# Reciprocal sums on a diagonal in the turning product, context tiles inside the last GLA head, and two stages that begin tile by tile of h

## What is computed

```python
p = softmax(scores)                      # MLA and NA: exp(s - max) / sum
out = einsum('bhqk,bkhd->bqhd', p, v)
h = x * (1 + sc1) + sh1                  # "plain" input of a layer of the second stack
x = layer_norm(alpha * x + g2 * mlp(x * (1 + sc2) + sh2))
merge(...) = concatenate([rms_norm(attn) * .., rms_norm(mem) * sigmoid(o)]) @ w_out   # even mixer
```

## Time and profile before

| | |
|---|---|
| median of 3 runs | 2934.42 us (2933.34 to 2937.86) |
| the profiled execution | 2933.31 us |
| its span in the profile | 2931.3 us |
| mean granted TensorE clock | 0.983 |
| TensorE busy | 2828.8 us, 97% of the span |
| VectorE busy | 2013.9 us, 69% |
| ScalarE busy | 1281.7 us, 44% |
| GpSimd busy | 339.3 us, 12% |
| chain that ended last | TensorE 80%, VectorE 11%, ScalarE 5% |

### The profile page before, as it was taken

The page is one execution under the profiler, slowest core; times in us unless marked ns, Lnnn a source line. Parts: engine busy times, 40 slices in busy tenths (PEclk is TensorE's granted clock), DMA queues, the critical chain, the costliest instruction groups (busy, mean ns, idle before and its releaser), DMA issues.

```text
span 2931.3 us, 44027 instructions
## 1 busy us (share of the span) xinstructions
PE 2828.8 (97%) x17694; PEld 2492.6 (85%) x17694; DVE 2013.9 (69%) x3397; ACT 1281.7 (44%) x2121; POOL 339.3 (12%) x380
## 2 busy tenths in 40 slices
PE   7999999998999999999999989999999999999998
PEld 6888898666888889888897889999979999887898
DVE  7789956555687656788655775666656689767764
ACT  4222244354422224222245565565455554645653
POOL 0000011322100001000011110022102210300100
PEclk8999999899999999999999999999999999999999
DMA  6666522011455534556432234455425579653453
GB/s 245 222 223 230 201 85 94 29 51 43 145 201 208 212 125 158 201 205 210 145 113 80 72 130 151 149 176 174 164 81 172 187 277 327 199 155 101 137 187 115
DMA packets 141194, 467.63 MB, mean 160 GB/s; under 512 B 27024, under 2 KB 29200, under 8 KB 140480
## 3 DMA queue, kind: packets, MB, share of 16 engines
q1 hardware_dynamic: 125440, 408.20, 41.2%
q0 software_dynamic: 15552, 56.63, 5.5%
HBM read 463.73 MB, written 1.05 MB: 159 GB/s over the span
## 4 chain that ended last, share of the span: by engine, by line
PE 80%; DVE 11%; ACT 5%; issue 2%; DMA 2%; POOL 1%; SPq 0%; ACTq 0%; DVEq 0%; POOLq 0%
PE bank L2657 24%; PE bank L2658 24%; PE bank L2659 24%; DVE sb_split_low L2061 3%; DVE sb_h_low L2148 1%; DMA sb_raw<-weights 1%; PE bank L2929 1%; PE bank L3100 1%; PE bank L2948 1%; DMA sb_ada_mlp<-ada 1%; DVE sb_temp L2075 1%; PE bank L2889 1%; DVE sb_x_res L2264 1%; DVE sb_temp L2142 1%; ACT sb_temp L1966 1%
## 5 line engine op out<-in xcount | busy, mean ns | idle before, releaser
L2657 PE MATMUL bank<-sb_h_high,sb_split_high 128*128 128x256 f32 (+1 forms) x3464 | 1116.6, 322 | 39.5 <-DVE sb_h_low L2156 16.5
L2658 PE MATMUL bank<-sb_h_low,sb_split_high 128*128 128x256 f32 (+1 forms) x3464 | 1097.8, 317 | 0.0
L2659 PE MATMUL bank<-sb_h_high,sb_split_low 128*128 128x256 f32 (+1 forms) x3464 | 1097.1, 317 | 0.0
L1646 ACT ACTIVATE sb_split_high<-sb_raw 128x1024 fp32r<-128x1024 f32 x620 | 646.4, 1051 | 306.6 <-PE bank L2659 286.2
L2061 DVE TENSOR_TENSOR sb_split_low<-sb_raw,sb_split_high 128x1024 fp32r<-128x1024 f32 x620 | 758.6, 1232 | 21.6 <-ACT sb_split_high L1646 21.5
L2657 PEld LDWEIGHTS bank<-sb_h_high,sb_split_high 128*128 128x128 f32 x3464 | 666.7, 192 | 100.9 <-issue 17.7
L2658 PEld LDWEIGHTS bank<-sb_h_low,sb_split_high 128*128 128x128 f32 x3464 | 667.8, 193 | 40.8
L2659 PEld LDWEIGHTS bank<-sb_h_high,sb_split_low 128*128 128x128 f32 x3464 | 667.0, 193 | 40.7
L2075 DVE CUSTOM_DVE_ANT_0 sb_temp<-sb_ada_ffn,sb_cond_ffn 128x1024 bf16<-128x1024 f32 x364 | 429.7, 1220 | 25.1 <-DMA sb_ada_ffn<-ada 16.0
L2657 PE MATMUL bank<-sb_hidden_high_ffn,sb_split_high 128*128 128x512 f32 (+1 forms) x830 | 280.4, 338 | 0.0
L2659 PE MATMUL bank<-sb_hidden_high_ffn,sb_split_low 128*128 128x512 f32 (+1 forms) x830 | 279.2, 336 | 0.0
(11 more groups left out here) (329 smaller groups left out, 3498.2 us busy)
## 6 DMA issues: line engine op xcount, KB each, us to landing
sb_raw<-weights SPq DMA_DIRECT2D x620, 512.0 KB, 3.4
sb_ada_ffn<-ada SPq DMA_DIRECT2D x114, 512.0 KB, 4.6
sb_ada_ffn<-ada POOLq DMA_DIRECT2D x90, 512.0 KB, 3.8
sb_ada_mlp<-ada POOLq DMA_DIRECT2D x18, 512.0 KB, 5.6
sb_ada_mlp<-ada SPq DMA_DIRECT2D x18, 512.0 KB, 5.9
sb_cond_ffn<-cond SPq DMA_DIRECT2D x3, 1024.0 KB, 5.4
sb_na_raw<-na_rpb SPq DMA_DIRECT2D x32, 96.0 KB, 6.8
sb_x_res<-tokens SPq DMA_DIRECT2D x4, 512.0 KB, 7.7
```

Source lines behind the costliest of these rows:

```text
L1646: do.activation(m.high[s % HIGHS][:, :], m.raw[s % RAWS][:, :], identity).then_inc(*act.mark("split_high", s))
L2657: do.matmul(out, ah, bh, start=start and j == 0, stop=False)
L2658: do.matmul(out, ah, bl, start=False, stop=False)
L2659: last = do.matmul(out, al, bh, start=False, stop=stop and j == len(terms) - 1)
```

## The change

Four edits. The weights of MLA and NA are no longer multiplied by the reciprocals. VectorE writes a 128 by 128 diagonal of them, and the turn is an ordinary float32 matmul with that diagonal as the moving operand. There is one diagonal for each c, so VectorE waits for the turn of the unit before. In the even mixer both spreads become a piece of their own, one unit later, and all four heads are put in unit 16. The context tiles 4 to 7 of cp00 move into units 22 to 26 of the GLA, into temps 0 to 3, and the first four pieces of `cmla_down` and of mlp1 are done tile by tile in four banks; n12 is then woven with the last three pieces only.

```diff
+def by_tile(pieces, ks=range(DT)):
+    for k in ks:
+        for first, *rest in pieces:
+            yield (*first, k, ks[0], ks[-1])
+            if k == ks[-1]:
+                yield from rest
...
-    extra[15] = extra[15] + [("even_put", "da", 0, j) for j in (0, 1)]
-    extra[16] = extra[16] + [("even_put", "da", 0, j) for j in (2, 3)]
+    extra[16] = extra[16] + [("even_put", "da", 0, j) for j in range(4)]
-    outs = [out_piece("even_out", k, 0, BOTH, ring) for k in range(4)]
-    outs += [[*even_spread("da", 0, j, ring), *out_piece("even_out", 4 + j, 0, BOTH, ring)] for j in range(2)]
-    outs += [out_piece("even_out", k, 0, BOTH, ring) for k in range(6, DT)]
+    outs = [out_piece("even_out", k, 0, BOTH, ring) for k in range(5)]
+    outs += [[step for j in range(2) for step in even_spread("da", 0, j, ring)]]
+    outs += [out_piece("even_out", k, 0, BOTH, ring) for k in range(5, DT)]
...
+    for i in range(4):
+        units[22 + i][0].append(("plain", "cp00", 4 + i, 0))
+        units[23 + i][0].append(("plain_put", "cp00", 4 + i, 0))
...
-    yield from flat([kept_warm(body[0], 9), *body[1:]])
+    yield "warm", 5, 9
+    yield from by_tile(body[:4])
+    yield from flat(body[4:])
...
-    tiles = plain_tiles("cp00", 0)
-    early = in_groups(tiles, (2,) * 7)
+    tiles = [(name, "cp00", k, 0) for name, k in skewed(4, ("plain", None, "plain_put"))]
+    early = in_groups(tiles, (2,) * 3)
-    yield from weave(down, [[], sums, [], spread, *tiles])
+    yield from by_tile(down[:4], (*range(4, DT), *range(4)))
+    yield from weave(down[4:], [sums, [], spread, *tiles])
...
+        self.diag = [self.ones, sb("diag", (P, P))]
...
+        if tag == "cp00" and k >= 4:
+            for d in range(2):
+                act.wait_ge("chunk_out", (2, d, N_CHUNKS - 1))
+        elif tag == "cp00":
+            act.wait_ge("h_low", (tag, k + 4, p))
...
         for c in range(2):
-            temp = m.temp[2 * (u % 3) + c][:, 0:n]
-            do.tensor_scalar(temp, temp, col[:, 4 + c:5 + c], None, ALU.mult)
+            if u:
+                dve.wait_ge("turned", (kind, u - 1, c))
+            do.tensor_scalar(m.diag[c][:, :], m.C("ident"), col[:, 4 + c:5 + c], None, ALU.mult)
...
-                last = do.transpose(m.bank[bank][:, kt * P:(kt + 1) * P], m.temp[2 * (u % 3) + c][:, kt * P:(kt + 1) * P], m.C("ident"))
+                last = do.matmul(m.bank[bank][:, kt * P:(kt + 1) * P], m.temp[2 * (u % 3) + c][:, kt * P:(kt + 1) * P], m.diag[c][:, :],
+                                 start=True, stop=True)
```

More of the change, by code:

```diff
@@ L1007, in order @@
     yield "gates", "odd_out"
+    yield "scales", "cp00"
     yield from flat(head[1])
@@ L1010, in order @@
     yield "scales", "n12"
-    yield "scales", "cp00"
     yield from beside_ffn11()
@@ L1387, in wait_for_x, with plain_temp @@
         lane.wait_ge("x_new", (src, k, p))
+def plain_temp(tag, k):
+    return k % (4 if tag == "cp00" else 5)
 def wait_for_h_free(lane, tag, p, k):
@@ L1710, in plain @@
         act.wait_ge("scales", tag)
-        if k >= 5:
+        if tag == "cp00" and k >= 4:
[3 more added lines that the diff above has]
+            act.wait_ge("h_low", (tag, k + 4, p))
+        elif k >= 5:
             act.wait_ge("h_low", (tag, k - 5, p))
-        do.activation(m.temp[k % 5][:, COLS[p]], m.x[:, k, COLS[p]], identity, scale=m.scales_of(tag)[:, k, p:p + 1],
+        do.activation(m.temp[plain_temp(tag, k)][:, COLS[p]], m.x[:, k, COLS[p]], identity, scale=m.scales_of(tag)[:, k, p:p + 1],
                       bias=m.mods[:, first + shift * DT + k, p:p + 1]).then_inc(*act.mark("plain", (tag, k, p)))
@@ L1722, in plain_put @@
         act.wait_ge("plain", (tag, k, p))
-        put_high(tag, k, p, m.temp[k % 5][:, COLS[p]])
+        put_high(tag, k, p, m.temp[plain_temp(tag, k)][:, COLS[p]])
     def layer_norm(tag, p, ks=range(DT)):
@@ L2159, in plain_put @@
     def plain_put(tag, k, p):
-        low_of(tag, k, p, m.temp[k % 5][:, COLS[p]])
+        low_of(tag, k, p, m.temp[plain_temp(tag, k)][:, COLS[p]])
         last_low[0] = tag, k, p
@@ L2578, in na_scores, with pair_normalise @@
         pair_max("na", u, T)
-    def pair_normalise(kind, u, n):
+    def pair_normalise(kind, u):
         col = m.cols[u % 6]
@@ L2585, in pair_normalise @@
         for c in range(2):
-            temp = m.temp[2 * (u % 3) + c][:, 0:n]
-            do.tensor_scalar(temp, temp, col[:, 4 + c:5 + c], None, ALU.mult).then_inc(*dve.mark("weights", (kind, u, c)))
+            if u:
+                dve.wait_ge("turned", (kind, u - 1, c))
+            do.tensor_scalar(m.diag[c][:, :], m.C("ident"), col[:, 4 + c:5 + c], None, ALU.mult).then_inc(
+                *dve.mark("weights", (kind, u, c)))
     def cmla_normalise(u):
-        pair_normalise("cmla", u, NC_TOK)
+        pair_normalise("cmla", u)
     def mla_normalise(u):
-        pair_normalise("mla", u, T)
+        pair_normalise("mla", u)
     def na_normalise(u):
-        pair_normalise("na", u, T)
+        pair_normalise("na", u)
     def weigh_put(kind, hd):
@@ L2664, in columns_of, with h_product @@
         return m.high[s % HIGHS][:, c], m.low[s % RAWS][:, c]
[L2666 to L2671, removed]
+    def h_product(bank, tag, s, p, keys, at=None, first=0, end=DT - 1):
+        if at in (None, first):
+            free(bank)
+            pe.wait_ge("split_low", s)
+        last = products(m.bank[bank][:, 0:T if p == BOTH else NC_TOK], [
+            (("h_low", (tag, k, p) if p in H_PARTS.get(tag, (0, 1)) else (tag, k)), *columns_of(s, k), *m.h_term(k, p))
+            for k in (range(DT) if at is None else (at,))], start=at in (None, first), stop=at in (None, end))
+        if at in (None, end):
+            last.then_inc(*pe.mark("gemm", *keys))
     def rstd_spread(tag, p):
@@ L2755, in small_sum, with up @@
         read[bank] = "mean", (tag, p)
-    def up(f, h, ab, p, bank):
+    def up(f, h, ab, p, bank, *at):
         s = PLACE[up_slab(f, h, ab)]
-        h_product(bank, H_OF[f], s, p).then_inc(*pe.mark("gemm", ("up", f, h, ab, p), s))
+        h_product(bank, H_OF[f], s, p, [("up", f, h, ab, p), s], *at)
         read[bank] = ("relu_squared" if n_up(f) == 1 else "hidden_raw" if ab else "silu"), (f, h, p)
@@ L2780, in down, with fm @@
         read[bank] = "x_new", ("x", f, c, k, p)
-    def fm(name, j, p, bank):
+    def fm(name, j, p, bank, *at):
         s = PLACE[fm_slab(name, j)]
-        h_product(bank, H_OF[name], s, p).then_inc(*pe.mark("gemm", ("fm", name, j, p), s))
+        h_product(bank, H_OF[name], s, p, [("fm", name, j, p), s], *at)
         read[bank] = fm_signal(name, j), (name, j, p)
@@ L2798, in out @@
         else:
-            s = PLACE[SLAB0[name] + k]
-            last = h_product(bank, tag, s, p)
-            keys.append(s)
+            assert False
         last.then_inc(*pe.mark("gemm", *keys))
```

## The result

The changed kernel takes 2945.73 us (median of 7 runs, 2942.75 to 2950.19) against 2936.98 us for the kernel before on the same chip (7 runs, 2933.34 to 2941.10). The ratio is 1.0036, with a 95% interval of 1.0025 to 1.0047: 10.6 us slower (7.3 to 13.8). The prediction had 2948.5 and "slower".

A forecast was written before the change was run, and what follows sets the result against it. TensorE, busy for 97% of the span, was taken as the bound, so added passes are paid wherever it never waits. 23.8 - 4.2 - 4.0 - 1.5 + 1.1 = +15.2 us on 2933.3 gives 2948.5, range 2936 to 2957.

The forecast's parts named there:

- The turn's records: Turn in cmla, MLA and NA: 448 records for 224 at 0.106 us each, 23.8 us more on TensorE.
- What NA absorbs: NA: 4.2 of TensorE's 7.6 us idle time come back, 2.6 in three waits and 1.6 in four late units.
- the prediction's last sentence: Forecast is wrong if the turns keep their pace, or if TensorE's idle time in NA falls to nothing.
- The new wait on VectorE: MLA: VectorE stands up to 2.8 us in three of eight units for the previous unit's turn; costed at nothing.
- That rival: VectorE's new wait becomes TensorE's: 8.4 us added in MLA, giving 2957; chance 0.11.
- The even mixer's end: Before 706: first and third of three waits go, 1.99 + 2.06 = 4.0 us gained; the middle 2.85 stays.
- The context's first projection: 1694 to 1737: 6.9 us won, 4.4 given back before ffn11, 1.0 off for moved work; 1.5 gained.
- The split does not stall: In cmla_down the low split has nothing before it but ScalarE's copy, so no stall.
- mlp1: Last feed-forward: 0.9 us won at the start, 2.0 stall before the fifth piece for a low split; loses 1.1.
- The turn is not free: Answers the rival that the turn costs no more than before, giving 2927.3, faster; chance 0.07.
- its plain matmul is not four transposes long: Answers the rival that the plain product is four transposes long: 71 us in place of 23.8, 2996; chance 0.02.
- The gains come in full: Rival: NA swallows 7.6 us, even mixer wins 10.1, projection 2.5, mlp1 even: +3.6, 2936.9; chance 0.12.

The follow-up runs named there:

- e6: Kernel before with each transpose of the turning product issued twice into the same place, VectorE's multiplications unchanged: ratio 1.0044, +12.9 us (9.4 to 16.7).
- e10: Kernel before with the turning product alone changed, but four diagonals in place of two, so VectorE waits for the turn two units before: ratio 1.0051, +15.0 us.
- e2: Kernel before with the even mixer's end alone changed (four puts in unit 16, both spreads as a piece of their own): ratio 0.9972, -8.2 us.
- e8: Kernel before with mlp1's first three pieces tile by tile, otherwise as before: ratio 0.9987, -3.8 us (-6.5 to -1.5).
- e4: Kernel before with the beginning of mlp1 alone changed (first four pieces tile by tile, nine warm matmuls on bank 5): ratio 1.0006, +1.8 us.
- e1: Kernel before with the turning product alone changed (diagonals, two-record matmuls): ratio 1.0052, +15.3 us (11.4 to 19.1).
- the single kernels: Four kernels, each the kernel before with one part of the change alone (turn, even mixer, context, mlp1): +15.3, -8.2, +0.9 and +1.8 us.
- e7: Kernel before with cp00 tiles 4 to 7 in the GLA, but cmla_down piece by piece and n12 woven as before: ratio 0.9976, -7.0 us.
- e9: Kernel before with the edits of e2, e7 and e8 together, the turn as before: ratio 0.9937, -18.5 us, median 2919.08 us.

## Why the prediction was right, step by step

The sign came out and the size roughly (+15.2 predicted, +10.6 measured). The turn's term was 4 us too high and the even mixer's gain 4 us too small, which both make the forecast too high; the context's term was 2 us too good and mlp1's 1 us, which hid part of it. That the sum lies no further off is to this extent luck, and one step, what NA absorbs, failed by a sign that the prediction itself had named.

- **The turn's records.** Right. 448 records, one more for each transpose. 23.8 us was predicted; at 0.117 us a record in MLA and 0.112 in NA, in place of 0.106, it is 3.8 + 7.5 + 14.3 = 25.6. A turn of MLA takes 1.81 us, where 1.6 to 1.7 was expected, in place of 0.85:

```profile
2136.91 1.16 PE L2918 MATMUL bank<-sb_ones,sb_temp 128*128 128x128 f32 x8
2137.91 1.06 PE L2918 MATMUL bank<-sb_diag,sb_temp 128*128 128x128 f32 x8
2138.72 0.36 PE L2684 MATMUL bank<-sb_h_high,sb_split_high 128*128 128x256 f32 x1
```

- **What NA absorbs.** The step that failed. 4.2 us was taken, of which 1.6 came from VectorE's saving; 7.6 us of idle time and 1.7 of lowered clock were absorbed, and e6 shows that VectorE's saving was not needed for it. TensorE's idle time in NA fell to nothing, which the prediction's last sentence names as a sign that it is wrong, and NA grew by 5.1 us where about 9 were expected. The prediction let each long wait take up only the 0.85 us of one unit's added records. But VectorE and ScalarE work on later units while TensorE is at this one: each unit of TensorE that gets longer gives them time for the next ones too, which would shrink every later wait until none is left. That reading is argued from the kernels and was not tried by itself. The upper bound of 7.6 was right for the idle time; it left out the clock.
- **The new wait on VectorE.** Right. It was put at up to 3 x 2.8 = 8.4 us in MLA and costed at nothing. (The shorter operation itself came as forecast: 284 ns in place of 484.) The changed kernel has 6.7 + 1.6 = 8.3 us of it there (groups of VectorE's instructions in MLA), and e10 shows that it costs nothing that can be told. That rival falls.

```profile
L2613 DVE TENSOR_SCALAR sb_ones<-sb_const,sb_cols 128x128 f32<-128x128 f32 x7 | 2.0, 286 | 6.9 <-PE bank L2918 6.7
L2613 DVE TENSOR_SCALAR sb_diag<-sb_const,sb_cols 128x128 f32<-128x128 f32 x7 | 2.0, 283 | 1.6 <-PE bank L2918 1.6
```

- **The even mixer's end.** Mis-sized: -4.0 predicted, -6.9 on average in the traces (four kernels with the edit at -6.8, seven without at +0.2), -8.2 (-11.7 to -4.7) in e2's timed runs. The wait of 2.85 us, which was to stay, went; an unforeseen one of 1.8 for the spread's bank came. Pieces and spreads take two banks in turn. Before, piece 4 lay between the spreads, so that the second had the bank of the first and waited for its scaling. Now piece 4 is ahead of both, and the second has the bank of piece 4 and waits for its addition. 5.1 us of idle time went in place of 4.0. Most of the rest is the clock. From 665 us in before to 723 the eight traces without the edit all have 6.9 us of idle time and those with it 1.8, while the clock costs 3.4 to 6.8 us (5.1 on average) in the eight and 1.7 to 3.4 (3.0) in the four: 2.1 us, by the granted clock in the timelines.
- **The context's first projection.** Too good by some 2 us: -1.5 predicted, +0.9 (-1.8 to +3.5) measured. The gain of 6.9 was 6.7 (5.2 in the changed kernel, where a lowered clock fell into it). The 4.4 given back were 5.4, for the reason stated (tiles at 0.78 us). "The split does not stall" in cmla_down was wrong, with waits of 0.39 and 1.32 us for low splits, though the gain held. The 1.0 for the work moved into the GLA is 0.7 in idle time: TensorE has 13.1 us of it in that stretch in the five kernels with the moved tiles and 12.4 in the seven without. In whole time the five are at +3.3 on average and the seven (before counted as 0) at +1.8; that difference is smaller than the scatter.
- **mlp1.** Right in mechanism: 2.0 us of stall predicted, 1.99 seen, for the low split and by the queue named. The gain at the start is 2.2 to 2.6 us with four pieces, the upper bound and not the 0.9 taken. The 0.9 supposed that the slow spell falls on the products, as it did before; where it did so (e8), the gain is 1.1, and in e4 it fell on the warm matmuls (last section). The stall's stretch costs 2.2 to 3.7 with the clock after it. Together -0.4 to +1.5 in traces and +1.8 (-0.9 to +4.4) in time, against +1.1.
- **The rivals.** The turn is not free (e1), and its plain matmul is not four transposes long but two (e1 against e6). The Trainium skill's factor of four for the transpose mode (page "TensorE: Matmul & The Clock Gate", section Terms) is not what this kernel sees: 0.109 us for a transpose against two records at 0.117, a factor of 2.1. "The gains come in full" was half right: NA swallowed its idle time whole and the even mixer gained 7, but the turn had 25.6 us of records and the projection gained nothing.

Measured by the single kernels, the terms are: turn 15.3 for 19.6, even mixer -8.2 for -4.0, projection +0.9 for -1.5, mlp1 +1.8 for +1.1. The differences, -4.3 - 4.2 + 2.4 + 0.7 = -5.4, are what separates 15.2 from 9.8, the sum of the four single kernels.

## What to carry to other kernels

Where TensorE is the bound, count its records first: here a float32 product with a diagonal has two for the one of a transpose, and what it takes off VectorE was worth nothing. An edit that changes the order of pieces moves two things, what they wait for and what they hide; e7 and e8 kept the first and left the second in place (n12's tiles beside four pieces, a split with a piece before it), and turned +0.9 and +1.8 into -7.0 and -3.8. In a pipeline of many like units such as NA here, where 13 to 14 us were added to a stretch with 7.6 us of short waits, take the whole idle time of TensorE as what added work will fill, with what its clock lost, and not a share of each wait.

## What the runs showed of the hardware

A spell of lowered clock does not fall on the same instructions in each execution. The code is the same in e4 and e8 up to mlp1's first product, and dense in both behind it. Nine warm matmuls (18 records) are followed by a wait for the first low part and then dense products. The table by stage of e4 and of e8, from 8 us before the first product:

```profile
2724.30:2732.30 8.00, 6.11 (x23) 4.82 (x22) 5.94 (x17) 5.54 (x13) 1.34 (x2) 0.79 0.00 1
2732.30:2740.30 8.00, 8.00 (x67) 8.00 (x68) 3.17 (x8) 4.48 (x12) 5.67 (x7) 1.00 0.01 2
```
```profile
2728.20:2736.20 8.00, 4.43 (x22) 3.64 (x23) 5.97 (x17) 5.51 (x13) 1.31 (x2) 1.00 0.00 1
2736.20:2744.20 8.00, 7.99 (x54) 8.00 (x55) 3.17 (x8) 4.50 (x12) 5.69 (x7) 0.79 0.01 2
```

Each has a mean of 0.79 in one of the two, which is 3.4 of 8 us at 1.2 GHz. In e4 it falls on the warm matmuls, for which nobody waits. In e8 it falls on the products, 54 records of which pass in place of 67, and the start gains 1.1 us in place of 2.6; e9, with e8's three pieces, has 2.6. One trace of such a stretch is good to about 2 us, and five timed rounds decide better. And an added transpose costs 0.109 us where an added record of the plain float32 product costs 0.117 (MLA; in NA 13.1 / 128 = 0.102 and 14.3 / 128 = 0.112), although the median duration of both reads 275 ns.
